# Two fused transformer blocks on one core: the SSD output loaded in three parts, the first gather in parts, an earlier load of a norm's scale

## The reference

```python
def _layer(...):                       # the first block
    h = modulate(rmsnorm(x)), modulate(rmsnorm(ctx))
    q, k, v, z, xbc, dt, g_na, g_ssd = split(h @ w_in)
    y_ssd = gated, normed state-space output, 512 x 2048
    y_na  = neighbourhood attention, 16 heads of 64, over x and ctx
    mix = (sigmoid(g_ssd) * (y_ssd @ w_branch_ssd)
           + sigmoid(g_na) * (y_na @ w_branch_na)) @ w_out
    x = x + gate1 * rmsnorm(mix)       # post-mix norm
    h2 = modulate(rmsnorm(x))
    scores = softmax(h2 @ w_router)    # 16 experts, each takes its 64 best rows
    for e in range(16):
        t = h2[rows of e]
        moe[rows of e] += weight * (silu(t @ w_gate[e]) * (t @ w_up[e])) @ w_down[e]
    x = x + gate2 * rmsnorm(moe)       # post-ffn norm
# then two layers of attention and a convolution-gated MLP
```

## Time and profile before

| what | value |
|---|---|
| median of the runs | 4125.56 us |
| the profiled execution | 4129.06 us |
| its span | 4127.3 us |
| PE matmuls busy | 3706.0 us (90%) |
| DVE busy | 1192.1 us (29%) |
| ACT busy | 703.3 us (17%) |
| POOL busy | 496.3 us (12%) |
| mean granted clock | 0.961 |
| read from HBM | 625.50 MB, 154 GB/s over the span |

### The profile page before, as it was taken

How to read it: one execution, slowest core, us unless ns; L and a number is a source line. 1 busy time by engine, 2 the same in 40 slices (tenths; PEclk the granted TensorE clock), 3 DMA queues, 4 the chain that set the end, 5 groups by cost and what they waited for, 6 DMA issues and landing times.

```text
span 4127.3 us, 32998 instructions
## 1 busy us (share of the span) xinstructions
PE 3706.0 (90%) x12728; PEld 1780.9 (43%) x12728; DVE 1192.1 (29%) x2718; ACT 703.3 (17%) x1446; POOL 496.3 (12%) x443
## 2 busy tenths in 40 slices
PE   6899998899899977888888888999999999999998
PEld 3455554444344433333333334544444445544443
DVE  2346655534300030211101014542221034422211
ACT  2023333222300120000000003321110013221100
POOL 1003234412000100000000002100221011012210
PEclk9899999999899989999999999999999999999999
DMA  7322223211122459999999991002221210122220
GB/s 247 122 86 61 79 61 101 73 27 59 46 92 82 169 207 409 409 409 409 409 409 409 409 393 60 31 21 82 82 82 66 87 51 31 41 69 74 82 77 31
DMA packets 301289, 634.08 MB, mean 154 GB/s; under 512 B 32403, under 2 KB 145667, under 8 KB 301007
## 3 DMA queue, kind: packets, MB, share of 16 engines
q1 hardware_dynamic: 239904, 591.96, 38.3%
q10 hardware_dynamic: 61231, 40.02, 3.5%
HBM read 625.50 MB, written 10.24 MB: 154 GB/s over the span
## 4 chain that ended last, share of the span: by engine, by line
PE 51%; DMA 18%; DVE 3%; ACT 1%; SPq 1%; issue 1%; POOL 1%; DVEq 0%; ACTq 0%; POOLq 0%
PE psum L295 27%; PE psum L2696 7%; DMA arena<-in_w_exp_up_dram 7%; DMA arena<-in_w_exp_gate_dram 6%; PE psum L1491 6%; DMA arena<-in_w_exp_down_dram 4%; PE psum L2286 3%; PE psum L1319 2%; PE psum L1347 1%; PE psum L1328 1%; PE psum L2235 1%; SPq L264 1%; PE psum L307 0%; DVE arena L1425 0%; PE psum L2206 0%
## 5 line engine op out<-in xcount | busy, mean ns | idle before, releaser
L295 PE MATMUL psum<-arena 128*128 128x512 f32 (+1 forms) x3392 | 1385.1, 567 | 7.2 <-POOL arena L1875 2.4
L295 PEld LDWEIGHTS psum<-arena 128*128 128x128 f32 x3392 | 648.7, 193 | 731.0 <-issue 705.2
L2286 PE MATMUL psum<-arena 128*64 128x512 f32 x3072 | 697.2, 600 | 147.3 <-DMA arena<-in_w_exp_up_dram 78.8
L2286 PEld LDWEIGHTS psum<-arena 128*64 128x64 f32 x3072 | 234.7, 137 | 591.6 <-issue 574.0
L1491 PE MATMUL psum<-arena 128*128 128x512 f32 x768 | 353.0, 615 | 0.8 <-DVE arena L521 0.8
L2696 PE MATMUL psum<-arena 128*128 128x512 f32 x704 | 303.0, 592 | 0.0
L710 PE MATMUL psum<-arena 128*128 128x512 f32 (+1 forms) x768 | 269.8, 511 | 1.3 <-ACT arena L533 1.3
L1491 PEld LDWEIGHTS psum<-arena 128*128 128x128 f32 x768 | 147.8, 196 | 192.7 <-issue 190.8
L2739 POOL TENSOR_SCALAR arena<-arena 128x512 f32<-128x512 f32 x88 | 137.5, 1563 | 718.2 <-ACT arena L2718 718.2
L1425 DVE CUSTOM_DVE_ANT_0 arena<-psum,arena 128x512 f32<-128x512 f32 (+3 forms) x224 | 114.0, 546 | 377.4 <-PE psum L1319 369.6
L2696 PEld LDWEIGHTS psum<-arena 128*128 128x128 f32 x704 | 133.5, 190 | 169.2 <-issue 169.2
(11 more groups left out here) (270 smaller groups left out, 2727.9 us busy)
## 6 DMA issues: line engine op xcount, KB each, us to landing
arena<-in_w_exp_gate_dram SPq DMA_DIRECT2D x128, 1024.0 KB, 18.6
arena<-in_w_exp_up_dram SPq DMA_DIRECT2D x128, 1024.0 KB, 18.5
arena<-in_w_exp_down_dram SPq DMA_DIRECT2D x128, 1024.0 KB, 18.6
arena<-in_w_in_dram SPq DMA_DIRECT2D x64, 1024.0 KB, 5.4
arena<-in_w_up_dram SPq DMA_DIRECT2D x88, 512.0 KB, 4.7
arena<-in_w_ada_dram SPq DMA_DIRECT2D x24, 1024.0 KB, 8.1
arena<-in_w_down_dram SPq DMA_DIRECT2D x20, 1024.0 KB, 4.9
arena<-acs_scratch ACTq DMA_DIRECT2D x64, 256.0 KB, 3.8
```

What stands on the lines that cost most here:

```text
L295: mm = pe.matmul(shaped(b, l, r), l, r, start=kt == 0, stop=kt == nkt - 1)
L2286: mm = pe.matmul(banks[n][64 * j:64 * j + 64, :], lhs[:, kt, 64 * j:64 * j + 64], w, start=kt == 0, stop=kt == 2 * nkb - 1)
```

## The change

Four things are changed.

1. `yT` becomes three parts in places that come free earlier: k-tiles 0 to 7 in new columns of their own at `PB` + 5632, 8 to 12 over Q and K of the even head groups, 13 to 15 over V of the first half. The rotation buffers move up by 4096 columns, `uT` lies where `HTn` was (its last readers are V's fillers). ACT waits for the last scores of head group 2 (unit 23), the last rotation and the values of pair 3, and asks for three transfers; one mark stands for all three. `PLAN1` has all 40 fillers within the steps.
2. The residual adds of tiles 0 to 2 behind `w_out` are DVE's, as for tile 3.
3. The first half of the first gather is two groups of 8 matmuls with a copy each: "a" ahead of the first expert's products, "b" behind its first block pair. The second half stays behind the second block pair.
4. The load of `gam2` is asked for by ACT in pair m = 6 (the seventh), behind its copies of the last gather, and no longer at the end. `logR` moves to a place apart from it.

```diff
+        yT_near = sb(o, 4096)
         ntmp = [...]
...
-        yT = r3(sb(PB, 8192), 512)
-        uT = r3(sb(PB + 8192, 4096), 512)
         o = FREE
+        uT = r3(sb(o, 4096), 512)
...
-        tmpE = [sb(o + 512 * i, 512) for i in range(2)]; o += 6144
+        yT_parts = [(0, 8, r3(yT_near, 512)), (8, 13, r3(sb(PB, 2560), 512)), (13, 16, r3(sb(o, 1536), 512))]
+        tmpE = [sb(o + 1536 + 512 * i, 512) for i in range(2)]; o += 6144
...
-                                   lambda i, kt, w: yT[:, kt, :], pool, "pe_branch")
+                                   lambda i, kt, w: y_tile(kt), pool, "pe_branch")
...
                     if half == 0 and n == 2:
-                        wait_all(act, [("full", ("s2", "na", 31, 1)), ("roped", ("na", 3, 3))])
-                        act.dma_start(yT, yD).then_inc(*up(S("yT_in"), ("yT",), by=16))
+                        wait_all(act, [("full", ("s2", "na", last_unit(NEAR.units, 2), 1)), ("roped", ("na", 3, 3)), ("full", ("o2", "na", 3))])
+                        for a, z, part in yT_parts:
+                            act.dma_start(part, yD[:, a:z, :]).then_inc(*up(S("yT_in"), by=16))
+                        mark(("yT",), S("yT_in"))
...
-        PLAN1 = [0, 2, 1, 1, 1, 1] + [1, 1, 1, 1, 1, 1] + [1, 1, 1, 1] + [1, 0] * 4 + [1, 0, 0, 0, 1, 0, 0, 0] + [0, 1, 1, 1, 1]
+        PLAN1 = [0, 2, 1, 1, 1, 1] + [1, 1, 1, 1, 2] + [1, 1, 1, 1, 0] + [1, 0, 1, 1, 0, 1] + [1, 1, 1, 1, 0] + [1, 2, 1, 2, 1, 2, 1, 2, 2, 2]
...
-                    if i == 3:
-                        dve.wait_ge(*now(S("dve_res")))
-                        dve.tensor_tensor(X[:, i, HALF[h]], X[:, i, HALF[h]], mix[:, i % 2, HALF[h]], ALU.add).then_inc(*up(S("dve_res"), ("X", "r1", i, h)))
+                    dve.wait_ge(*now(S("dve_res")))
+                    dve.tensor_tensor(X[:, i, HALF[h]], X[:, i, HALF[h]], mix[:, i % 2, HALF[h]], ALU.add).then_inc(*up(S("dve_res"), ("X", "r1", i, h)))
...
-            pool.wait_ge(*at("X_in"))
-            for i in range(3):
-                for h in range(2):
-                    pool.wait_ge(*at("mg", "r1", i, h))
-                    pool.tensor_tensor(X[:, i, HALF[h]], X[:, i, HALF[h]], mix[:, i % 2, HALF[h]], ALU.add).then_inc(*up(S("pool_res"), ("X", "r1", i, h)))
...
-        logR = sb(SB + 4096, 512)
+        logR = sb(MS, 512)
...
+        GATHER = {0: (0, 4), 1: (4, 8), "a": (0, 2), "b": (2, 4)}
...
         def dve_gather(dve, m):
-            key = ("xg", m, 0)
-            dve.wait_ge(*at("full", key))
-            dve.tensor_copy(xgb[:, 0:4, :], r3(PS.of(key), 128)).then_inc(*up(S("dve_xg"), ("free", key), ("xgs", m, 0)))
+            for q_ in ("ab" if m == 0 else (0,)):
+                key = ("xg", m, q_)
+                a, z = GATHER[q_]
+                dve.wait_ge(*at("full", key))
+                dve.tensor_copy(xgb[:, a:z, :], r3(PS.of(key)[:, 0:128 * (z - a)], 128)).then_inc(*up(S("dve_xg"), ("free", key), ("xgs", m, q_)))
...
         def pe_experts(pe, m):
-            pe.wait_ge(*at("xgs", m, 0))
+            pe.wait_ge(*at("xgs", m, 0 if m else "a"))
...
-                        if s == 0 and wn == "g" and kb == 1:
-                            if m == 0:
-                                pe_gather(pe, 0, (1,))
+                        if s == 0 and wn == "g" and kb < 2 and m == 0:
+                            pe_gather(pe, 0, (1 if kb else "b",))
+                            pe.wait_ge(*at("xgs", 0, 1 if kb else "b"))
+                        elif s == 0 and wn == "g" and kb == 1:
                             pe.wait_ge(*at("xgs", m, 1))
...
+            if m == 6:
+                act.dma_start(gam2, gamD[1:2, :].rearrange("a n -> (a n)").partition_broadcast(128)).then_inc(*up(S("gam2_in"), ("gam2",), by=16))
...
         def act_moe_end(act):
             act.dma_start(gcon, gsrc).then_inc(*up(S("gcon_in"), ("gcon",), by=16))
-            act.dma_start(gam2, gamD[1:2, :].rearrange("a n -> (a n)").partition_broadcast(128)).then_inc(*up(S("gam2_in"), ("gam2",), by=16))
...
-            pe_gather(pe, 0, (0,))
+            pe_gather(pe, 0, ("a",))
```

More of the change, by code:

```diff
@@ L1805, in sp_branch_ssd, with y_tile @@
             sp_gates(sp, "n", CGN, 0)
+        def y_tile(kt):
+            a, _, part = next(p for p in yT_parts if p[0] <= kt < p[1])
+            return part[:, kt - a, :]
         def pe_branch_ssd(pe, pool):
@@ L2198, in pe_gather @@
                 b = open_bank(pe, ("xg", m, q_), PALL)
-                for kt in range(4):
+                a, z = GATHER[q_]
+                for kt in range(a, z):
                     for i in range(4):
-                        if q_ == 0 and kt == 0:
+                        if q_ in (0, "a") and kt == 0:
                             pe.wait_ge(*at("Pm", m, i))
@@ L2204, in pe_gather @@
                                 pe.wait_ge(*at("h2", i, 1))
-                        c0 = (4 * q_ + kt) * 128
-                        mm = pe.matmul(b[:, kt * 128:(kt + 1) * 128], h2[:, i, c0:c0 + 128], Pb[:, i, :], start=i == 0, stop=i == 3)
+                        mm = pe.matmul(b[:, (kt - a) * 128:(kt - a + 1) * 128], h2[:, i, kt * 128:(kt + 1) * 128], Pb[:, i, :], start=i == 0, stop=i == 3)
                 mm.then_inc(*up(S("pe_xg"), ("full", ("xg", m, q_))))
```

## The result

The changed kernel takes 4091.7 us (median; 4088.4 to 4097.1) against 4124.1 us of the kernel before on the same chip (4118.1 to 4127.1), a ratio of 0.9925 [0.9907, 0.9942]. Forecast were 4095.4 us, between 4085 and 4110, and a gain of 30.2 us; 32.4 us came. The two profiled executions differ by more, 4127.3 and 4090.9 us of span.

What follows compares the result with a forecast made beforehand. PE, busy for 90% of the span, was taken as the bound, losing time to holes and low clock. Terms -27.4 - 1.5 + 0.3 - 1.6 = -30.2 us took the median 4125.56 to 4095.4 us, range 4085 to 4110.

Steps and rivals of the forecast that it cites:

- Part one: Neighbourhood attention: fillers in all steps cut PE's holes and slow work from 42.6 to 15.2 us, saving 27.4 us.
- the four steps named: Attention steps 15, 17, 20 and 26, without a filler ahead under the new plan: holes of 9.1 us together.
- One price for every hole: Attention: each PE hole brings 1.5 us of slow work, so the four remaining holes bring 6.1 us.
- rival B: Attention: no slow work behind the four lonely holes; -36.3 us, 4089.3 us; chance 0.09.
- Rival A: Attention: clock stays low though PE is full, only 18.4 us come; -21.2 us, 4104.4 us; chance 0.11.
- Rival C: Attention: sigmoids or evictions waiting for fillers delay exponentials, filled steps keep holes; slower, 4151 us; chance 0.04.
- Rival D: Load comes late or experts' weight stream takes the saving back, nothing of part one seen: 4123 us; chance 0.04.
- The cover of the load: Between third gate and first SSD output product PE has 18.5 us of work against 0.7 + 12.6, hiding the yT load.
- Part two: Residual adds of tiles 0 to 2: DVE instead of POOL shortens the chain by 0.47 us each, -1.5 us.
- Part three: First gather in parts: pair 0 ends 2.1 us earlier, everything from pair 1 on 0.3 us later, so +0.3 us.
- the danger that I had named: First gather: the new first hole might hold the low clock down, costing 3.5 us more.
- Part four: Second norm's scale loaded with pair seven: DVE starts 2.9 us earlier, bytes cost the stream 1.3 us; together -1.6 us.

Runs made afterwards that it cites:

- no_holes: Changed kernel with a filler in every attention step but the first and the yT load split differently, each part with its own semaphore: 4073.6 us, ratio 0.9885.
- gates_by_copy: Changed kernel with Copy in place of Sigmoid in the eight gates: 4097.0 us in one execution, attention stage 581.2 us.
- attention_only: Changed kernel with parts two to four undone, so part one alone: 4091.1 us, ratio 0.9922 to the kernel before.
- load_without_cover: Changed kernel with the three yT transfers asked for behind the fourth gate instead of the third: attention stage 594.8 us, 17.3 longer.
- rest_only: Changed kernel with part one undone (old places, one load, old plan), parts two to four kept: 4121.9 us, ratio 0.9993 to the kernel before.
- new places: Changed kernel with the old plan and parts two to four undone, leaving only the three yT places and split load: 4126.5 us, ratio 1.0016.

## Why the prediction was right, point by point

**Part one, -27.4 forecast, -30.7 in the two profiles, -29.0 without the wait for POOL.** The mechanism held: the holes at L1328 went where a filler came before the step, and stayed at exactly the four steps named, with 9.4 us (9.1 forecast). The waits fell by 26.0 + 1.4 - 9.4 = 18.0 us, where I had 18.4. So 12.7 us came from slow work, where I had 15.1 - 6.1 = 9.0: that is the mis-sized term. 1.7 of the 12.7 are those behind the wait for POOL, which neither my sum nor the change touches. The other 11.0 are in the steps. Against `no_holes` the kernel before has 608.2 - 564.5 = 43.7 us, of which 27.4 are waits and 1.7 lie behind POOL, so its holes carried 14.6 of slow work (15.1 forecast); in the profile after, four holes carried 3.6 (6.1 forecast). The rows at 1020.01 and 1077.79 show that 3.6 in another way: 1.75 us behind each of two holes (turns 1.2 and 1.0 too long, and 0.55 and 0.8 on the scores and values behind them), and nothing behind 976.82 and 990.18. One price for every hole was the wrong model: rival B was right for two of the four, and my 1.5 us somewhat low for the others.

How well the size was hit is partly luck of the execution. In part one alone and with the gates by Copy the same four holes carried some 5 us, about the 6.1 of the forecast, and the stage took 581.2. Other programs with the old plan took 605.4 and 615.0. Between single profiles the new plan is worth 24 to 38 us in this stage, and 27.4 and 30.7 can't be told apart by them.

**Rival A** (the clock stays low though PE is full) is refuted by 1.00 over 200 us in `no_holes`; here it was 0.98, with the low stretches behind two of the holes. **Rival C** (ACT and DVE take over as the bound) falls with `gates_by_copy`: no hole in a filled step, with sigmoids or without. **Rival D** falls with `attention_only`: part one alone has the whole gain, so the experts' stream did not take it back; it starts earlier by what the attention saves.

**The cover of the load** held. I counted 18.5 us against 13.3 and up to 3 more. PE came to its product 19.2 to 20.1 us after the requests, and the last data 13.6 us after the first request, where the one load before took 12.6. So at most 1 of the feared 3 us for the fourth weight block came. The price without cover, a microsecond each, is that of `load_without_cover`, with the clock's 2.4 us on top.

**Part two, -1.5 forecast, -1.5 measured** (57.6 to 56.1, as in `rest_only`): 3.37 to 2.90 us in three tiles.

**Part three, +0.3 forecast, +1.0 to +1.2 measured.** Pair 0 starts 2.2 us earlier behind the gather (4.28 us instead of 6.50; 2.1 forecast) and ends 1.8 earlier, and nothing of it comes back: the third block pair starts 19.01 us behind the gather (1448.18 to 1467.19), and in the kernel before 18.06 (1485.74 to 1503.80, the row below from PE's timeline), so it is 0.95 late.

```profile
1503.80 2.37 PE L2286 MATMUL psum<-arena 128*64 128x512 f32 x10 [0.25 <-ACT arena L2222]
```

0.35 of that is the second hand-over, as in the sum. 0.46 is the low clock, the danger that I had named and not priced in: the clock was still 0.65 from 1452 to 1454, and pair 0's first 16 records take 4.12 us where the second 16 take 3.66. With the whole gather, pairs 0 and 1 have 7.10 for 32. The full 3.5 us of my upper bound did not come. Over all twelve profiles the third block pair starts 17.7 to 18.3 us behind a whole gather and 18.6 to 19.0 behind one in parts, 0.7 later in the mean, and in `rest_only` pair 0 has no slow record at all. So 0.7 of the 1.0 to 1.2 us is seen at the third block pair; where the rest of it comes from, if it is more than the scatter of the stretch, no run shows.

**Part four, -1.6 forecast, -2.1 to -2.3 measured.** DVE starts 2.9 us earlier, as worked out. The bytes in the full stream were charged at 1.3 us, and the last experts lose 1.0 from the third block pair to the last down block (its start moves by -35.59 us while the third block pair moves by -36.61). That makes -1.9 by this pair of profiles, and -2.1 to -2.3 by the two by two. The 1.0 scatters: this stretch is 943.8 to 944.6 us in three profiles with the scale asked for late (before, part one alone, new places), and 944.5 to 946.2 in seven with the early one.

**The sum.** -30.7 - 1.5 and -0.9 for the experts are -33.1 us against -30.2, and the medians give -32.4. The 36.4 of the two spans would have read as a larger success of the steps than there was: 5.3 of them lie before the first instruction that the change touches, and 1.7 behind the wait for POOL.

## What to carry to other kernels

Where an engine waits for a chain over other engines at every step, independent work of that engine, spread so that no step is without it, buys back more than the waits: here 9.4 us of holes carried 3.6 us of slow work besides in one profile and some 5 in another, and 27.4 us of holes carried 14.6. Before an early start of a piece is counted as a gain, look for what sets the end: pair 0 came 2.2 us earlier and the experts' stretch got about 1 us longer by it. And measure stages between landmarks, with the unchanged stages as the control, before a difference of two profiles is put down to a change.

## What was not expected of the hardware

The same holes bring different amounts of slow work. With the old plan the attention stage took 608.2, 605.4 and 615.0 us in three programs; PE stood for 27.4, 27.4 and 27.8 us of them from 900 to 1145 us. With four holes it took 577.5, 581.2, 581.2, 577.7 and 577.5 us. With none it took 564.5 in all three. The spread goes with the holes. In the rows of the changed kernel the holes of 2.79 us (976.82) and 2.21 (990.18) are followed by turns at full speed, and those of 2.16 and 1.89 us by turns at half: so the length of a hole did not decide.

Nor did its place in the program. The hole of 2.15 us at step 20 carried 1.75 us of slow work in the changed kernel, 3.3 with the gates by Copy and none in the run without cover. The wait of 2.43 us for POOL, with the same work behind it, carried 1.7 us in four of twelve profiles and nothing in eight. No run settled what does.

A load of an ACT function table, 1.28 us, was hidden at a lag of two steps whether there were five of them in the stage or thirteen.
